# TensorE's side pieces placed by an account of all engines, and the delta rule's norm moved beside the dilated units

## What is computed

```
def first_block(x, ...):
    xn = rmsnorm(h, norm_mix)
    dq, dk, dv, dz, da, db, aq, ak, av, gate_dn, gate_da = split_columns(xn @ w_in, IN_WIDTHS)
    o_dn = rmsnorm(delta_rule(both directions), out_norm) * silu(dz)
    o_da = dilated_attention_branch(aq, ak, av, rel_bias)
    merged = sigmoid(gate_dn) * (o_dn @ w_branch_dn) + sigmoid(gate_da) * (o_da @ w_branch_da)
    h = h + merged @ w_out
    h = h + peer_ffn(rmsnorm(h, norm_ffn), w_q, sub_keys, expert_u, expert_v)

def second_block(x, c, ctx, c_ctx, ...):
    for i in range(2):
        mod = silu(c) @ w_mod[i] + b_mod[i]          # six rows that scale, shift and gate
        h = rms_norm(x) * (1 + sc1) + sh1            # the same for the context tokens
        x = x + g1 * (concat(gla, neighbourhood, window) @ w_out)
        x = x + g2 * swiglu(rms_norm(x) * (1 + sc2) + sh2)
    return rms_norm(x, final_norm)
```

## Time and profile before

| | us |
|---|---|
| median of 3 runs | 4268.33 |
| profiled execution | 4268.82 |
| its span | 4267.0 |
| TensorE busy with matmuls | 3885.8 |
| VectorE busy | 2390.1 |
| ScalarE busy | 1686.0 |
| mean granted clock of TensorE | 0.952 |

### The profile page before, as it was taken

One profiled execution on the slowest core, in us unless ns is written; L12 is line 12 of the kernel. 1 busy time (PEld: TensorE's weight loads), 2 busy tenths in 40 slices (PEclk: granted clock), 3 DMA queues, 4 the chain that ended last, 5 costly groups with the idle time before them and its releaser, 6 DMA issues. The chain is left out here.

```text
span 4267.0 us, 57393 instructions
## 1 busy us (share of the span) xinstructions
PE 3885.8 (91%) x23037; PEld 3355.6 (79%) x23037; DVE 2390.1 (56%) x4212; ACT 1686.0 (40%) x2807; POOL 728.7 (17%) x580
## 2 busy tenths in 40 slices
PE   7899998988898789999999999887899999778998
PEld 4677876676798779999999999665677777567887
DVE  4344323455788767777777776555543335554333
ACT  3422332344356783333333333435432232444222
POOL 0012000152205423322222232100000010101000
PEclk8999999999999899999999999988899999879999
DMA  5311234432244449888888885311134341102332
GB/s 202 117 46 35 66 96 148 177 109 71 87 154 168 137 177 300 290 281 280 281 279 286 283 278 186 101 50 44 52 129 137 115 142 60 62 24 65 99 95 78
DMA packets 209193, 617.30 MB, mean 145 GB/s; under 512 B 18464, under 2 KB 68640, under 8 KB 205088
## 3 DMA queue, kind: packets, MB, share of 16 engines
q1 hardware_dynamic: 168352, 465.76, 33.8%
q0 software_dynamic: 40576, 147.87, 9.9%
HBM read 583.67 MB, written 29.88 MB: 144 GB/s over the span
## 5 line engine op out<-in xcount | busy, mean ns | idle before, releaser
L463 PE MATMUL ps<-hhi,whi 128*128 128x512 f32 (+1 forms) x2824 | 1098.8, 389 | 34.1 <-ACT whi L421 19.1
L429 DVE TENSOR_TENSOR wlo<-raw,whi 128x1024 fp32r<-128x1024 f32 x576 | 714.1, 1240 | 717.8 <-ACT whi L421 710.1
L465 PE MATMUL ps<-hlo,whi 128*128 128x512 f32 (+1 forms) x2824 | 1065.0, 377 | 0.3
L421 ACT ACTIVATE whi<-raw 128x1024 fp32r<-128x1024 f32 x660 | 694.2, 1053 | 655.9 <-PE ps L474 501.5
L474 PE MATMUL ps<-hhi,wlo 128*128 128x512 f32 (+1 forms) x2824 | 668.9, 375 | 0.0
L463 PEld LDWEIGHTS ps<-hhi,whi 128*128 128x128 f32 x2824 | 542.7, 192 | 139.4 <-issue 46.0
L465 PEld LDWEIGHTS ps<-hlo,whi 128*128 128x128 f32 x2824 | 543.3, 192 | 73.8 <-issue 7.0
L474 PEld LDWEIGHTS ps<-hhi,wlo 128*128 128x128 f32 x2824 | 513.6, 189 | 72.1 <-issue 4.8
L465 PE MATMUL ps<-ag_lo,whi 128*128 128x384 f32 x1024 | 342.6, 335 | 0.0
L463 PE MATMUL ps<-ag_hi,whi 128*128 128x384 f32 x1024 | 342.5, 334 | 0.0
L429 POOL TENSOR_TENSOR wlo<-raw,whi 128x1024 fp32r<-128x1024 f32 x85 | 206.4, 2436 | 326.7 <-ACT whi L421 325.1
(11 more groups left out here) (629 smaller groups left out, 6118.7 us busy)
## 6 DMA issues: line engine op xcount, KB each, us to landing
raw<-w_in SPq DMA_DIRECT2D x151, 512.0 KB, 3.6
raw<-peer_u SPq DMA_DIRECT2D x128, 512.0 KB, 4.6
raw<-peer_v SPq DMA_DIRECT2D x128, 512.0 KB, 4.2
raw<-w_mod SPq DMA_DIRECT2D x96, 512.0 KB, 4.2
raw<-w_gate SPq DMA_DIRECT2D x66, 512.0 KB, 3.5
raw<-w_up SPq DMA_DIRECT2D x66, 512.0 KB, 3.5
raw<-w_down SPq DMA_DIRECT2D x66, 512.0 KB, 3.5
gate_dram<-stage SPq DMA_DIRECT2D x24, 1024.0 KB, 4.6
```

What stands on the lines that cost most here:

```text
L421: a.x.activation(whi[n % NW][:], raw[i % NRAW][:], ACT.Copy, bias=0.0, scale=1.0).then_inc(*a.gives("hi", i))
L429: e.x.tensor_tensor(wlo[n % NW][:], raw[i % NRAW][:], whi[n % NW][:].bitcast(F32), ALU.subtract).then_inc(*e.gives(*lo_sig(i)))
L463: t.x.matmul(o, w, p.hi, start=grp.opens and k == 0, stop=False)
L465: t.x.matmul(o, w, p.lo, start=False, stop=False)
```

## The change

1. The account. Every engine's instructions, waits and signals are noted as they are placed (`Clocked`), and `settle` plays them forward: an instruction costs what it cost before, a table load 1.28 us, a wait ends 0.06 us after its signal, a DMA takes its bytes at 380 GB/s and 2.2 us.
2. `Ready(signals)` holds a stream until the account expects the signals, and `coming(ring, ...)` also those that free the PSUM bank it will take. It stands ahead of nearly every side piece, and the delays after pieces become 0.3 us. `drain` takes the stream that is expected first.
3. `split_ahead` is called after every tick, not once in a unit, and splits a slab only once the account has it landed.
4. The 16 blocks of `w_mod` of layer 0 that were strewn among 11 convolution units become 8 there and 8 among the last 12 units `da`.
5. `finish` becomes three parts: `unit_o` (norm of the delta rule) starts when both chains end, `oda` (splitting of the dilated result) follows the heads, and the gate is applied in the evacuation of the `z` units. The load of the residual `xres` on SyncE's queue waits for that gate (`z_v`), no longer for the chains.
6. Some streams get one more `yield`, so that ScalarE's and VectorE's instructions of a step stand behind the step's matmul.

```diff
+    def expected(self, signals):
+        return max([self.ready.get(s, 1e9) for s in signals], default=0.0)
...
+                    if kind == "wait":
+                        self.clock[e] = max(self.clock[e], self.ready.get(what, 0.0) + 0.06)
+                    elif kind == "work":
+                        self.clock[e] += what
+                    elif kind == "give":
+                        self.ready[what] = self.clock[e] + (0.2 if e == "tensor" else 0.03)
+                        coming.discard(what)
+                    else:
+                        self.wire = max(self.wire, self.clock[e]) + more[0] / 380e3
+                        self.ready[what] = self.wire + 2.2
...
+    def coming(ring, *signals, n=1):
+
+        r = rings[ring]
+        return Ready(*signals, *[f for j in range(n) for f in freed.get(r[(turn.get(ring, -1) + 1 + j) % len(r)], ())])
...
-                yield 3.2
+                yield 0.3
+                yield coming(ring, (cw, "nl", step), (cw, "it", step), n=2)
...
-                yield 4.0
+                yield 0.3
+                yield Ready(("attend_a", it.key, "exp", 1))
+                yield 0.0
                 yield from pick(t, lane, "turn", it)
                 note(t, "turn", it, True)
+                yield Ready(("attend_v", it.key, "weights"), ("attend_a", it.key, "weights"), *frees(group_of["turn", it.key]))
...
+                yield coming("key", ("dense_a", n, "gated"), ("dense_v", n, "b"))
                 b = take(t, "key", ("dense", n), ("dense_a", n, "out"))
...
-    spine += u_dn[:2] + coupled(u_dn[2:], m0[:32]) + u_da + u_z + u_merge[:2]
+    spine += u_dn[:2] + coupled(u_dn[2:], m0[:16]) + u_da[:-12] + coupled(u_da[-12:], m0[16:32]) + u_z + u_merge[:2]
...
+    def here(i):
+        return i < NRAW or plan.expected([(f"raw{i % NRAW}", (i,))]) <= plan.now()
+
     def split_ahead(i):
-        while sum(n > i for n in unsplit) < LOOK and split_next():
+
+        while sum(n > i for n in unsplit) < LOOK and here(at_unit["split"]) and split_next():
             pass
...
     plan.drain("dilated")
-    run(2)
-    plan.drain()
     plan.put("do", "xres")
-    plan.start("finish", streams["finish"])
-    run(2 * GL - 2)
-    plan.drain()
-    run(24 - 2 * GL)
+    run(24)
```

More of the change, by code:

```diff
@@ L120, in nothing, with activation, dma_start @@
         return self
-    activation = tensor_tensor = tensor_scalar = scalar_tensor_tensor = tensor_copy = memset = work
+    def activation(self, out, in_, function, **k):
+        if function in (ACT.Exp, ACT.Ln, ACT.Silu, ACT.Sigmoid, ACT.Sqrt, ACT.Gelu_apprx_tanh) and function != self.table:
+            self.table = function
+            self.spent += 1.28
+        return self.work(out)
+    def dma_start(self, out, in_):
+        n = 4
+        for x in out.shape:
+            n *= x
+        self.moved += n
+        return self
+    tensor_tensor = tensor_scalar = scalar_tensor_tensor = tensor_copy = memset = work
     copy_predicated = tensor_tensor_reduce = reciprocal = tensor_tensor_scan = work
@@ L134, in indirect_dma_start, with __init__, note, wait_ge @@
         return self
+class Clocked(Seat):
+    def __init__(self, tally, name, raw):
+        super().__init__(tally, name, raw)
+        self.notes, self.seen = collections.deque(), 0.0
+    def note(self, *what):
+        if self.x.spent > self.seen:
+            self.notes.append(("work", self.x.spent - self.seen))
+            self.seen = self.x.spent
+        if what:
+            self.notes.append(what)
+    def wait_ge(self, flag, *key):
+        self.note("wait", (flag, key))
+    def gives(self, flag, *key, step=1):
+        given = super().gives(flag, *key, step=step)
+        if step < 16:
+            self.note("give", (flag, key))
+        else:
+            self.note("land", (flag, key), self.x.moved)
+            self.x.moved = 0.0
+        return given
 class When:
@@ L263, in drain @@
         while any(n in self.side for n in names or list(self.side)) and not (until and until in self.placed):
[L264 to L267 removed]
+            at = {n: max(self.due[n], self.expected(self.blocked[n].signals) if isinstance(self.blocked[n], Ready) else 0.0)
+                  for n in self.side if isinstance(self.blocked[n], Ready) or not self.held(n)}
+            n = min(at, key=at.get, default=None)
+            assert n and at[n] < 1e9, ("nothing can go on", list(self.side))
+            self.clock["tensor"] = max(self.clock["tensor"], at[n])
+            self.held(n)
             self.step(n)
@@ L643, in gpsimd @@
             else:
[L644 removed]
+                for c in range(KC if self.tap else KC - 1):
                     yield
@@ new lines, in unit_o_scalar, with oda_tensor, oda_scalar @@
+            yield
+    streams["unit_o"] = {"tensor": unit_o_tensor, "vector": unit_o_vector, "scalar": unit_o_scalar}
+    def oda_tensor(t):
+        for h in range(4):
+            yield When(("da_head", h))
+            yield 2.0
+        yield 0.0
+    def oda_scalar(a):
+        for h in range(4):
+            a.wait_ge("da_v", "oda", h, 3)
+            for d in range(2):
+                a.wait_ge(f"chain{d}_v", "out", 3)
+            a.x.activation(oda_hi[:, h], oda[:, h], ACT.Copy, bias=0.0, scale=1.0).then_inc(*a.gives("oda_a", h))
+            yield
+        yield
@@ L1562, in program, with oda_vector @@
+    def oda_vector(v):
+        yield
+        for h in range(4):
+            v.wait_ge("oda_a", h)
+            v.x.tensor_tensor(oda_lo[:, h], oda[:, h], oda_hi[:, h].bitcast(F32), ALU.subtract).then_inc(*v.gives("oda_v", h))
+            yield
+    streams["oda"] = {"tensor": oda_tensor, "vector": oda_vector, "scalar": oda_scalar}
     gate = [sb(f"gate{i}", WK + 82 + 2 * i, [T]) for i in range(6)]
@@ L2531, in tensor @@
             for y in range(2):
+                yield coming("lat" if i else "key", m.there("nv", i))
                 if i:
@@ L3671, in program, with chain_end @@
     run(11)
-    plan.start("prep", streams["prep"], then=lambda: [plan.start(f"chain{d}", streams[f"chain{d}"]) for d in range(2)])
+    plan.put("do", "gchain")
+    def chain_end():
+        if not {"chain0", "chain1"} & set(plan.side):
+            plan.start("unit_o", streams["unit_o"])
+            plan.start("oda", streams["oda"])
+    plan.start("prep", streams["prep"],
+               then=lambda: [plan.start(f"chain{d}", streams[f"chain{d}"], then=chain_end) for d in range(2)])
     plan.start("dilated", streams["dilated"])
```

362 lines of the change are left out of this document (218 added, 144 removed).

## The result

The changed kernel takes 4092.06 us (median of 4 runs, 4082.31 to 4096.30) against 4269.44 us for the kernel before in the same comparison: a ratio of 0.9581, with a 95% interval of 0.9564 to 0.9599. That is 177 us less, where 128 were forecast. The profiled execution is the quickest of the four, 4082.31 us with a span of 4080.5 us; so the two profiles differ by 186.5 us, 9 more than the medians.

The account below looks back on a forecast made before the run. TensorE was taken as the bound, by its work, 381 us of idle time and its clock. Terms -24 -16 -14 -12 -8 -54 = -128 took 4268.8 to 4141 us, range 4080 to 4250.

Parts of the forecast that it names:

- Up to unit 57: Three terms at the kernel's start: w_mod loads -24 us, norms, chunks and dilated attention -16, finish stage -14.
- The finish stage's units: Finish stage: 15.5 us of waits and 4 us of clock go, one more drained dilated item costs 5; sum -14 us.
- the norms and chunks: Norms, chunks and dilated attention to 490 us: 14 us of idle time and 2 us of clock go, -16 us.
- the first term: Beside the convolution: with one w_mod block ahead of a unit, waits for slabs go, -24 us (bounds -28 to +10).
- Router beside the context's attention: Router scores stop waiting for a bank that VectorE still reads: 9 us and 3 us of clock, -12 us.
- 1097 to 1597 us: Router, SwiGLU and gate table: 25 more drained dense items add 41 us, units ahead lose 29 and 20; -8 us.
- Latent layers: Two latent layers, each -27 us: first stretch -3, second net -18 (drained near attention adds 26), third -6; two -54.
- The drains cost more: Rival, chance 0.12: bare drains behind latent projections and of dense items outweigh the saved waits; slower, 4300 us.
- Only what has a mechanism of its own pays: Rival, chance 0.22: only loads (-24) and norm (-14) pay, elsewhere waits move from piece to piece; 4231 us.
- The account errs as often as the delays did: Rival, chance 0.04: the account is no better than fixed delays, and drains add all that the rest saves; 4268 us.
- The clock gives back more: Rival, chance 0.10: 60% of 252 us at the lower clock goes, each worth half, 76 us for 49; 4114 us.
- The clock terms: Parts of the terms won from TensorE's clock rising in stretches with side streams; the prediction put them at 49 us.

Follow-up runs that it names:

- Experiment 1: The changed kernel with its 16 strewn blocks of w_mod put back among the 11 convolution units: 4106.7 us, ratio 0.9611.
- Experiment 2: The kernel before with the spreading of w_mod alone, all delays as before: 4267.4 us, ratio 0.9993.
- experiment 4: The changed kernel with the dilated stream at its old delays, and the router and gate table without gates: 4112.8 us, ratio 0.9631.
- Experiment 7: The changed kernel with the attention lanes (near, window, context) at their old delays and no Ready: 4150.6 us, ratio 0.9720.
- experiment 9: The changed kernel with drain picking the stream that is due first, among those that can go on: 4113.2 us, ratio 0.9635.
- experiments 7 and 8: The second of these: the changed kernel with GLA at its old delays and no Ready in all four layers: 4120.7 us, ratio 0.9649.
- experiment 6: The changed kernel with Ready always satisfied, so each side piece is placed once its 0.3 us are over: 4190.3 us, ratio 0.9809.

## Why the prediction was right, and where it was off

The forecast was 4141 us with a range of 4080 to 4250; 4092 lies within it, 49 us below the centre. Most of the signs came: beside the convolution there is no wait for a slab and a clock of 0.98, the wait of 11.6 us for `osq` and GLA's waits over 3 us for `l_tmp` are gone, and the drain of 36 dense items is 62 us long. One didn't: the stretch of latent layer 0 is 54.8 us shorter, not 20 to 35. In the order of its steps, by the profiles (which differ by 186.5 us):

- **Up to unit 57** (-24 -16 -14 = -54): measured 672.4 to 618.8, -53.6. The sum holds and its parts shift. The start up to unit 13 got 37.6 us shorter, of which 9 us are moved matmuls (17.5 us of them before, 8.5 now): 28.6 against 24. The finish stage's units lost 19.8 us, where the forecast has 15.5 + 4 (its 5 us for one more drained item fall into the units before). Units 13 to 36, the norms and chunks, took 330.4 us for 344.2: 13.8 gained where I had 16. Units 36 to 53 took 155.8 for 138.2, with 8.5 us of `w_mod` and 2.4 of the norm moved in, which leaves 6.7 us for the drained item and what the blocks stir up there. Experiment 1 shows that the first term is the spreading's; two blocks ahead of one unit as its reason is borne out by where the waits stood, and not by a run. But I took it that a block beside the last units `da` meets nobody. Experiment 2 shows the contrary for the order before: alone, the spreading gives nothing. The term was right only because other parts of the same change cover it.
- **Router beside the context's attention** (-12, bounds -22 and 0): measured -28.3, outside its bounds. I took the lower bound to be the idle time alone. It went almost wholly (20.9 us), and 7.4 us of clock with it (0.91 to 1.00). The 18.6 us behind line 2895 in the earlier trace rows have "issue" for a releaser, so no row names the bank as their cause; the waits are gone with `coming` and without it some are back (2.2, 1.3 and 3.9 us in experiment 4).
- **1097 to 1597 us** (-8): measured -2.9. The drain of 36 dense items cost 40.4 us more (forecast 41) and the units ahead of it gave 43 (forecast 49). VectorE works 399 and ScalarE 323 of the 500.6 us, but TensorE works 416. The new waits for slabs behind ScalarE (28.5 us for 13.2) are 15 us that the forecast didn't see. By the rule on the most contended engine (the Trainium skill, "Perfetto Trace Analysis", "Identifying the Most-Contended Engine"), as the prediction read it, the term was 0; the measured one lies between it and mine.
- **Latent layers** (-27 each): measured -54.8 and -49.6. This is the step that failed in size, and it makes 50 of the 58 us by which the profiles' difference exceeds the forecast; the router's 16 and the smaller terms, some of them the other way, leave 8. The first stretch gave 7 us (forecast 3), the second 24.7 (forecast 18), and the third 23.1 where I had 6. There I saw 17.0 us idle at a clock of 0.83 and counted neither that the gates would remove the waits for the softmax for the most part (11 us) nor that the clock would then go to 1.00 (12 us). Experiment 7 shows that 12.9 us of the 23.1, waits and clock together, belong to the lanes' gates. In the second stretch idle time fell by 15.8 us, although 174 instructions more are drained; the forecast had 30 saved and 26 lost, so 4. The clock gave 8.9 us there, where it had 14. Picking the stream that is expected first is worth 4.8 us there and 6.0 in the third stretch (experiment 9), and I hadn't priced it at all. Such parts overlap and aren't a sum.
- **Unforecast**: units 57 to 111 took 5.5 us more; the wait for the key table among them grew from 3.9 to 7.1 us.

The rivals. *The drains cost more*: no; the drained near attention costs, but its stretch is shorter than before. *Only what has a mechanism of its own pays*: refuted by experiments 7 and 8. *The account errs as often as the delays did*: no, by 177 us. *The clock gives back more*: it was right in the share and wrong in the price. It wanted 60% of the 252 us at the lower level to go from the stretches with side streams; by the same reading of the windows (length times twice what the clock lacks to 1) they hold about 85 us now, so two thirds went. But each was worth less than half. Over the whole kernel time at the lower level fell from 2 x 0.048 x 4267 = 410 to 2 x 0.027 x 4080 = 220 us, by 190, and TensorE's busy time by 67, that is 0.35 for one. The Trainium skill ("TensorE: Matmul & The Clock Gate", "Terms") puts those 190 us at 95, an estimate; this case's traces don't bear it out, because TensorE idles through part of the slow time. It worked for 291 of the 410 us and works for 146 of the 221; half of the 145 between them is 73, near the 67. So what is worth half is the busy part of the slow time alone.

Two terms of the prediction's text don't add up. The clock terms that it states are 8, 2, 4, 3 and twice 14, together 45 and not 49. And 30 of 42.5 us, "the same share" of 23 us of clock, are 16 and not 14. Neither moves the forecast by more than 4 us.

What stays open: which of the finer pieces, the shorter delays and the choice of banks by the account makes the 27 and 24 us that the latent layers gain without any gate (experiment 6) was not taken apart. That is about half of what these layers gain in all.

## What to carry to other kernels

In this kernel, a planner that knows when inputs are due was worth most where many short streams meet in one engine's queue, and it paid twice: the wait went, and the clock of the work around it rose. Parts of a rescheduling aren't additive by nature; a move that frees one stretch (the blocks of `w_mod`) can be worth nothing until the place that it goes to can bear it, so test it alone and with the rest. Look last for what the account leaves out, and for what it puts into another engine's queue: a slab's split behind a waiting instruction of ScalarE's made TensorE wait 6 us, and one DMA issued in the same piece as its user made TensorE wait 7 us, in a stretch that then gained 14.

## What the runs showed of the hardware

- Short pauses can cost as much in clock as in idle time. In the window lanes' stretch of layer 0 17.0 us of idle time, mostly in waits of 1.5 to 2.3 us, went with a clock of 0.83, and 531 matmul instructions took 81.3 us; with 5.9 us idle the clock is 1.00, and they take 69.3 us.
- Idle time alone doesn't set the clock. The drain's stretch of a layer idles 26 us of 128 at a clock of 0.85, while the gate table's drain idles 19 us of 62.1 at 0.97. The gate table's waits there are short (18.8 us in 32 waits, one of them 3.4), in the layer's drain four are over 4 us. That this makes the difference is likely and was not tested.
- The clock in a stretch varies though the work and the idle time don't: units 49 to 53 took 48.6 us in the change's profile (clock 0.93) and 49.2 to 51.9 in those of six of its variants (0.91 to 0.84), all with 9.5 us idle there. Over whole executions of one program, the change's, it was 0.970 to 0.973. So a stretch of one profile is good to some 3 us.
- Time at the lower clock costs only where TensorE works in it: 190 us less of it, 145 of them worked through, took 67 us off the same 23037 matmul instructions.
- The account's 1.28 us for a table load of ScalarE's is nearly its whole price. Of the 79 loads of the changed kernel, each 1.28 us, 57 have under 1.5 us (1.31 as a rule) between the end of the instruction before and the start of the one after.
